# Where four subtractions run: splitting the residual into bf16 parts on VectorE alone

## The reference

```python
def pool_mixer(x, pool_w, pool_scale):
    ...                       # trailing mean over w positions minus the token, w = 2, 4, 8, 16
    y = jnp.einsum("bsgc,gcd->bsgd", pooled, pool_w).reshape(B, S, D)
    return y * pool_scale

def reference(x, norm_mix, norm_ffn, ...):
    h = x
    for i in range(DEPTH):
        if i < N_A_LAYERS:
            h = h + pool_mixer(rmsnorm(h, norm_mix[i]), pool_w[i], pool_scale[i])
        else:
            j = i - N_A_LAYERS
            if j == 0:
                k, v = shared_kv(h, kv_norm, w_kv, k_norm)
            h = h + stick_breaking_layer(rmsnorm(h, norm_mix[i]), k, v, w_q[j], q_norm[j], w_o[j])
        h = h + hier_moe(rmsnorm(h, norm_ffn[i]), moe_w_grp[i], ...)
    return h
```

## Time and profile before

| | us |
|---|---|
| median of 3 runs (lowest, highest) | 1440.48 (1440.04, 1441.68) |
| profiled execution | 1440.64 |
| its span on the core | 1438.8 |
| TensorE busy | 1352.4 (94%) |
| VectorE busy | 562.9 (39%) |
| ScalarE busy | 423.1 (29%) |
| GpSimd busy | 41.4 (3%), 35 instructions |
| moved from HBM | 478.86 MB, mean 334 GB/s |

### The profile page before, as it was taken

How to read it: one execution, slowest core, us unless ns; L and a number is a source line. 1 busy time by engine, 2 the same in 40 slices (tenths; PEclk the granted TensorE clock), 3 DMA queues, 4 the chain that set the end, 5 groups by cost and what they waited for, 6 DMA issues and landing times.

```text
span 1438.8 us, 22979 instructions
## 1 busy us (share of the span) xinstructions
PE 1352.4 (94%) x9239; PEld 771.9 (54%) x9239; DVE 562.9 (39%) x910; ACT 423.1 (29%) x629; POOL 41.4 (3%) x35
## 2 busy tenths in 40 slices
PE   8899999998998988999999999989999999889896
PEld 7554444443334436888888887774444434334343
DVE  3832232232222326756566655552223313223132
ACT  3511111111111115575656565441111111111110
POOL 0300000000000000101000000010000000000000
PEclk8999999999999998999999999999999999999999
DMA  9969999999999999554554543568999999999996
GB/s 322 370 277 383 421 421 422 422 422 422 422 422 422 422 410 340 178 179 146 176 175 147 175 152 137 179 239 350 385 420 421 422 421 422 422 422 421 422 422 238
DMA packets 95446, 481.69 MB, mean 335 GB/s; under 512 B 9266, under 2 KB 9348, under 8 KB 45988
## 3 DMA queue, kind: packets, MB, share of 16 engines
q1 hardware_dynamic: 94804, 477.58, 83.7%
q10 hardware_dynamic: 432, 2.88, 0.5%
q0 software_dynamic: 160, 0.52, 0.1%
HBM read 478.86 MB, written 2.10 MB: 334 GB/s over the span
## 4 chain that ended last, share of the span: by engine, by line
issue 53%; PE 23%; DMA 16%; DVE 4%; ACT 2%; POOL 1%; SPq 0%; POOLq 0%; DVEq 0%; ACTq 0%
DMA ring<-in_moe_w_up 16%; PE ps L1350 9%; PE ps L1215 6%; PE ps L1382 3%; PE ps L1292 1%; POOL head_rs L506 1%; DMA const<-in_constant_table 1%; PE ps L1332 1%; DVE ws L782 1%; PE ps L1441 1%; ACT ws L522 1%; ACT parts L538 1%; PE ps L1333 0%; DVE xr L810 0%; PE ps L1452 0%
## 5 line engine op out<-in xcount | busy, mean ns | idle before, releaser
L1350 PE MATMUL ps<-ring,xg 128*64 128x512 f32 x1968 | 447.1, 596 | 44.9 <-DMA ring<-in_moe_w_up 42.5
L1215 PE MATMUL ps<-ws,xs 128*128 128x512 f32 x1632 | 383.2, 394 | 5.7 <-DVE xs L1160 2.4
L1215 PEld LDWEIGHTS ps<-ws,xs 128*128 128x128 f32 x1632 | 304.3, 189 | 74.5 <-DVE ws L782 4.2
L1350 PEld LDWEIGHTS ps<-ring,xg 128*64 128x64 f32 x1968 | 143.9, 137 | 318.1 <-issue 308.6
L1382 PE MATMUL ps<-ring,hidT 128*64 128x512 f32 x1024 | 226.8, 596 | 0.0
L967 DVE TENSOR_TENSOR y_lo<-ps,y_hi 64x512 fp32r<-64x512 f32 x128 | 88.1, 688 | 218.9 <-ACT y_hi L574 215.9
L785 DVE SCALAR_TENSOR_TENSOR ws<-ring,vecs,ws 128x512 fp32r<-128x512 f32 x192 | 134.4, 748 | 89.4 <-ACT ws L525 89.4
L563 ACT ACTIVATE silu_g<-ps,slot_scale 64x512 f32<-64x512 f32 x32 | 21.8, 683 | 459.5 <-PE ps L1350 459.5
L525 ACT ACTIVATE ws<-ring,vecs 128x512 fp32r<-128x512 f32 x192 | 127.4, 716 | 92.5 <-PE ps L1215 84.6
L947 DVE TENSOR_TENSOR resid<-resid,ps 128x512 f32<-128x512 f32 x128 | 82.5, 685 | 170.5 <-PE ps L1333 170.5
L574 ACT ACTIVATE y_hi<-ps 64x512 fp32r<-64x512 f32 x128 | 75.7, 591 | 239.1 <-PE ps L1382 236.8
(11 more groups left out here) (160 smaller groups left out, 665.2 us busy)
## 6 DMA issues: line engine op xcount, KB each, us to landing
ring<-in_moe_w_down SPq DMA_DIRECT2D x128, 1024.0 KB, 21.8
ring<-in_moe_w_up SPq DMA_DIRECT2D x124, 1024.0 KB, 23.7
ring<-in_moe_w_gate SPq DMA_DIRECT2D x122, 1024.0 KB, 22.3
ring<-in_w_kv SPq DMA_DIRECT2D x32, 1024.0 KB, 5.4
ring<-in_w_q SPq DMA_DIRECT2D x16, 1024.0 KB, 5.1
ring<-in_w_o SPq DMA_DIRECT2D x16, 1024.0 KB, 5.0
extra<-in_moe_w_gate SPq DMA_DIRECT2D x6, 1024.0 KB, 8.4
ring<-in_pool_w SPq DMA_DIRECT2D x4, 1024.0 KB, 16.8
```

The lines of the kernel that those rows point to most:

```text
L1215: last = mm(ps[:, bank + t, :], xs[:, px, k, cols], ws[:, b, pw, j, :], start=(first and j == 0 and n == 0), stop=(last_unit and j == 1 an ...
L1350: last = mm(ps[CAP * h:CAP * h + CAP, b, :], xg[:, b, k, :], both[h][:, j, :], start=(k == 0), stop=(k == KD - 1))
```

## The change

VectorE takes over every left and every third, of both tiles and both layers. In the mixer its order for a block is left, third for tile 0, and then left, third for tile 1. In the output projection the second left stands directly behind the first, between units 10 and 11 of each block, and the two thirds behind unit 12. In block 3 of either layer third of tile 0 stands behind the mean square and third of tile 1 behind the second left, both ahead of the wait for the power. GpSimd keeps the power (`inverse_rms`, and that of the heads) and the two loads. No buffer, transfer or product changes.

```diff
@@ GpSimd
-            def left(l, c):
-                if l + c:
-                    pool.wait_ge(lo_done[1], NBLK * l + c)
-                    pool.wait_ge(mid_done[1], NBLK * l + c)
-                pool.wait_ge(resid_added, (0, ADD_O)[l] + 2 * c + 2)
-                nc.gpsimd.tensor_tensor(rest_tiles(1), resid_tiles(1, c), resid_top(1, c),
-                                        ALU.subtract).then_inc(rest_done[1], 1)
-            def third(l, c, t):
-                pool.wait_ge(rest_done[t], NBLK * l + c + 1)
-                nc.gpsimd.tensor_tensor(in_tiles(2, t, c), rest_tiles(t), rest_top(t),
-                                        ALU.subtract).then_inc(lo_done[t], 1)
-            def residual_parts(l):
-                for c in range(NBLK - 1):
-                    left(l, c)
-                    third(l, c, 1)
-                third(l, NBLK - 1, 0)
-                inverse_rms(2 * l + 1)
-                third(l, NBLK - 1, 1)
...
-            residual_parts(0)
+            inverse_rms(1)
             inverse_rms(2)
...
-            residual_parts(1)
+            inverse_rms(3)
@@ VectorE
-            def third(l, c):
-                dve.wait_ge(rest_done[0], NBLK * l + c + 1)
-                nc.vector.tensor_tensor(in_tiles(2, 0, c), rest_tiles(0), rest_top(0),
-                                        ALU.subtract).then_inc(lo_done[0], 1)
+            def third(l, c, t):
+                dve.wait_ge(rest_done[t], NBLK * l + c + 1)
+                nc.vector.tensor_tensor(in_tiles(2, t, c), rest_tiles(t), rest_top(t),
+                                        ALU.subtract).then_inc(lo_done[t], 1)
...
                 mean_square(2 * l + 1, False)
+                third(l, NBLK - 1, 0)
                 left(l, NBLK - 1, 1)
+                third(l, NBLK - 1, 1)
                 dve.wait_ge(rs_done, 2 * l + 2)
...
                     router_rows(0, g - 1)
-                    left(0, g - 1, 0)
-                    third(0, g - 1)
+                    for t in range(NT):
+                        left(0, g - 1, t)
+                        third(0, g - 1, t)
...
                     o_unit(8 * c + 10)
                     left(1, c, 0)
+                    left(1, c, 1)
                     o_unit(8 * c + 11)
                     o_unit(8 * c + 12)
-                    third(1, c)
+                    third(1, c, 0)
+                    third(1, c, 1)
                     o_unit(8 * c + 13)
```

## The result

The changed kernel takes 1446.62 us (median of 8 runs, 1445.28 to 1449.16), the kernel before 1441.26 (8 runs, 1440.04 to 1442.06). The ratio is 1.0037, with a 95% interval of 1.0028 to 1.0046: slower by 5.4 us. The forecast was 1446.8 and a loss of 6.2. Four of the eight runs lie between 1445.28 and 1446.16 and four between 1447.08 and 1449.16, so the median falls into the gap between them. The profiled execution took 1445.80 us with a span of 1443.9, against 1440.64 and 1438.8.

A forecast was written before the change was run, and what follows sets the result against it. Experts were taken as transfer-bound, projections as TensorE-bound, and VectorE's chain as what delays the gather. Layer 0's 4.3, the output projection's 0.95 and layer 1's tail 0.9 sum to 6.15 us: 1446.8 us, range 1445.4 to 1448.3.

The forecast's parts named there:

- the power's turn: Tails of both layers: GpSimd's power and VectorE's subtractions take turns, so the power's 0.57 us adds to VectorE's chain.
- What bounds the kernel: Experts bound by transfers, projections by TensorE; delays of the token gather move the ring load at 87.85 us one to one.
- rival 3: Layer 0 is cover: transfers are what is late at 88 us, only layer 1's 1.9 us counts, 1442.5; chance 0.06.
- Blocks of the mixer: Layer 0, blocks 0 to 2: the added subtractions delay VectorE by 1.05, 1.74 and 1.62 us, 4.41 us in all.
- Logits and tail of layer 0: Logits 4.12 us later; with the power's turn the tail ends at 78.65, slot_of at 83.2 instead of 78.9, +4.3.
- sign of 1.5 us or more in both tails: Tails of both layers: the power would take 1.5 us or more if the forecast were right.
- The rule that the prediction cites: Trainium skill: a VectorE instruction with two SBUF inputs and a GpSimd instruction reading SBUF exclude each other; issue order decides.
- Output projection: Second left ahead of unit 11 makes its weights 0.32 us late for TensorE in each of three blocks, +0.95; thirds hidden.
- Tail of layer 1: Third, left, third on VectorE plus the power's turn delay the logits by 0.9 us, or 0.25 without turns.
- Rival 1: No turns, no stall: the power slips in and TensorE doesn't feel the 0.32; +4.4 us, 1445.0; chance 0.17.
- Rival 2: Half clock from TensorE's longer waits in the tails reaches gather or first expert: +2.5, together 8.7, 1449.3; chance 0.12.
- Rival 4: Faster: GpSimd no longer holds VectorE up in block 0, added instructions fall into gaps; -0.9 us, 1439.7; chance 0.03.

The follow-up runs named there:

- e4: Changed kernel with the last mixer unit's weights (ScalarE copy, VectorE subtraction) ahead of the parts of block 0 instead of behind them; ratio 1.0031 to the kernel before.
- e10: Kernel before with only the two thirds of block 3 in each layer on VectorE, the rest of tile 1 staying on GpSimd; ratio 0.9995.
- e5: Changed kernel with unread products of constants in TensorE's waits between the router's products of blocks 1, 2 and 3; 1448.21 us, ratio 1.0050 to the kernel before.
- e7: Changed kernel with 40 unread products of constants in TensorE's wait ahead of unit 6 of the output projection; 1447.42 us, ratio 1.0038 to the kernel before.
- e3: Changed kernel with the second left of each output projection block behind unit 11 instead of ahead of it; 1444.43 us, ratio 1.0022 to the kernel before.
- e8_best: Kernel before with work moved off VectorE to GpSimd, last mixer unit first, ScalarE's first parts later, constant products in TensorE's waits; 1437.06 us, ratio 0.9966.

## Why the prediction was right, step by step

The direction, the size and the place of the loss were right; one step, the power's turn, was wrong in both tails, and the others were off in size.

**What bounds the kernel.** Right. The expert stretch kept its rate and length, and the ring load came 3.71 us later, seen from the first left, exactly as slot_of did (82.00 to 90.95 is 8.95, as before from 78.90 to 87.85). From there to the power ahead of the attention it is 478.83 us, before 478.67. The delay passed one to one, so rival 3 falls.

**Blocks of the mixer.** Forecast +1.05, +1.74, +1.62, sum 4.41; measured +1.03, +1.71, +1.56, sum 4.30. e4 shows how the first came about: with the unit's weights ahead of the parts the block is as short as before (5.78 us against 5.76), so it was ScalarE's wait for the second left, as the prediction had it, and not VectorE's load.

**Logits and tail of layer 0.** Forecast +4.12 for the logits without the power and +4.6 with it; measured +4.08. The power didn't decide. The step by which the power "must get its turn among them" and adds its 0.57 us failed: e10 and the changed kernel both show the power wait for the one instruction under way, end beside the next, and slow it by nothing. So the power takes 1.09 and 1.07 us, and the forecast's sign of 1.5 us or more in both tails didn't come. The rule that the prediction cites, by which the two exclude each other, doesn't show in the left beside the power (1.07 us, as alone). Slot_of was forecast at +4.3 and came at +3.71: the rest of the gap, 0.37, is in the clock products, 4.68 us instead of 5.05. I had taken them as fixed, and they took 2.84 (e5) to 5.29 us (e4); in e7, with the same order and 5.01 us for them, A is 4.03 above before.

**Output projection.** Forecast 3 x 0.32 = 0.95; measured 1.10 from addition to addition, 0.37 in each block. The mechanism is shown by e3, which takes it all back.

**Tail of layer 1.** Forecast +0.9 by the power's turn; measured +0.10, in the changed kernel and in e10. The forecast had +0.25 without turns, and even that was too much: from the first addition of block 3 to the logits it is 6.79 us (962.29 to 969.08), before 6.67, so VectorE was late by about a tenth.

**The sum.** 3.71+1.10+0.10 = 4.9 us by the chains, against 6.15 forecast and 5.4 measured between the medians. So two terms were too high by 0.6 and 0.8 and one too low by 0.15. The two profiled executions are 5.2 us apart: to the 4.9 come stretches that the change doesn't touch, 0.6 less ahead of the first left and 0.8 more behind, of it 0.6 in expert layer 1. The forecast was built on a profiled execution of 1440.64, and its counterpart took 1445.80, 1.0 us less than forecast. That the median of 1446.62 is within 0.2 us of 1446.8 is luck: it lies in the gap between the four short and the four long runs. Rival 1 (4.4) was nearer to the 4.9. Its first half, a power that adds nothing, is what the runs show; its second half, a TensorE that doesn't feel the 0.32, is not.

**Rival 2, the clock.** In this execution the clock did fall in the tail of layer 1, to 0.50, where it had been 1.00:

```profile
970.00:971.00 1.00, 1.00 (x13) 1.00 (x11) 0.86 (x6) 0.15 (x1) 0.00 (x0) 0.50 1.03 426
```

It lay on clock products under VectorE's chain (4.36 us instead of 2.84) and was back at 1.00 for the gather, so it cost nothing there. In e4, with the same order in layer 1, they took 2.84. The clock's price shows elsewhere, in D, 1.5 us in three of twelve profiles, where the change does nothing. **Rival 4** falls with the 1.43 gone and the time longer.

## What to carry to other kernels

Before moving work between engines, ask what each engine's chain releases: here VectorE was busy for 40% of the time, and yet each added pair of subtractions in the mixer (1.74 us) cost 1.03 to 1.71 us, since in those 25 us VectorE's chain, with one wait for ScalarE, set when the transfer-bound stretch could start. In a busy stage, place matters more than amount: one subtraction of 1.06 us cost 0.37 us in each block of the output projection ahead of a unit, and nothing behind it. And where a limit is removed, look for the one just under it; here it was a row of clock products, which let through 0.54 of the 1.16 us that e4 had gained before it.

## What the runs showed of the hardware

- GpSimd and VectorE are not held up alike. A power of 2 elements waits for the VectorE instruction under way (1.07 to 1.55 us instead of 0.69) and doesn't delay the next (1.07 us beside it). Subtractions of 512 elements on GpSimd do delay VectorE's: 1.43 instead of 0.69, 1.93 instead of 1.07, and 1.08 instead of 0.20 for 40 elements. VectorE's additions with an input in `ps`, TensorE's results, kept their 0.69 us beside them (60.81 in e8_best, while GpSimd ran from 60.83 to 62.88).
- The same wait of 2.37 us on TensorE ended at full clock in five of eight profiles, and in three with some microseconds at 0.50, 1.5 us longer in all (24 products in 7.36 instead of 5.76 us). With 40 products in the wait it did not occur in four profiles, which can be chance. Three other stretches vary by 1.8 to 2.2 us without a known cause. Together these are about as large as the difference that was to be measured.
- 48 products of 128x128 whose results nobody reads took 2.84 us at a granted clock of 1.00 (e5), and 4.36, 4.68, 5.05 and 5.29 us where it was 0.50 for a part of them.
